# Scores in pieces of 512 keys, transposed rows as one transfer, first weights in the gather ring: one change to a one-core inference step

## The reference, cut to what matters

```
h = rmsnorm(x) * g1;  z = h @ w_in                        # D = 1024, w_in is 1024 x 3096
GLA heads (4): gated linear attention with a decaying state; output normed, times silu(gate)
FoX heads (8 of 64): s = q.k/8 + c_q - c_k (c = running sum of log forget gates), causal softmax, @ v
x = x + concat(GLA, FoX) @ w_out
PEER: q = rmsnorm(x)*g2 @ w_q (8 heads); scores of 2 x 128 subkeys, top 16 of each, top 16 of the 256 sums;
      idx -> rows u, v of 16384 experts;  x = x + sum over 128 picks of softmax(top)*gelu(u.h)*v
```

## Time and profile before

| what | us |
|---|---|
| median of 3 runs (3266.09 to 3274.44) | 3267.21 |
| the profiled execution | 3259.53 |
| its span, first to last instruction | 3257.7 |
| first gather issued, after the start | 149.0 |

### The profile page before, as it was taken

How to read it: one execution, slowest core, us unless ns; L and a number is a source line. 1 busy time by engine, 2 the same in 40 slices (tenths; PEclk the granted TensorE clock), 3 DMA queues, 4 the chain that set the end, 5 groups by cost and what they waited for, 6 DMA issues and landing times. The chain is left out here.

```text
span 3257.7 us, 34318 instructions
## 1 busy us (share of the span) xinstructions
PE 2673.6 (82%) x9396; PEld 1587.3 (49%) x9396; DVE 2528.8 (78%) x5522; ACT 1489.3 (46%) x3922; POOL 1290.6 (40%) x1062
## 2 busy tenths in 40 slices
PE   7768788886987888787977898888887898888777
PEld 5647456443753455444643455444643446444322
DVE  2498887999668768997677777998668766888864
ACT  2252463454235744454245654444245663444532
POOL 0024333443344434334443443444444434444443
PEclk9789758998998999998988899998998999988889
DMA  6499988999999999999999899999999999999998
GB/s 219 153 410 398 375 328 340 421 421 404 398 421 398 420 395 395 418 415 394 421 417 374 354 407 410 415 421 404 422 418 380 415 369 406 416 420 418 408 421 352
DMA packets 193753, 1269.82 MB, mean 390 GB/s; under 512 B 23720, under 2 KB 36792, under 8 KB 43032
## 3 DMA queue, kind: packets, MB, share of 16 engines
q0 software_dynamic: 152064, 1107.36, 83.4%
q1 hardware_dynamic: 36712, 154.26, 11.9%
q10 hardware_dynamic: 4784, 6.01, 0.6%
HBM read 1258.55 MB, written 9.00 MB: 389 GB/s over the span
## 5 line engine op out<-in xcount | busy, mean ns | idle before, releaser
L734 POOL DMA_INDIRECT uv_ring<-in_peer_uv,expert_index x1056 | 1285.8, 1218 | 1944.3 <-PE ps_acc L1301 1491.6
L1301 PE MATMUL ps_acc<-uv_ring,coef_diag 128*128 128x512 f32 x2744 | 1455.7, 672 | 451.1 <-ACT coef_diag L1000 430.5
L1662 DVE CUSTOM_DVE_ANT_0 uv_ring<-uv_ring,h_rows 128x1024 f32<-128x1024 f32 x1056 | 1281.7, 1220 | 357.5 <-DMA uv_ring<-in_peer_uv,expert_index 347.9
L1301 PEld LDWEIGHTS ps_acc<-uv_ring,coef_diag 128*128 128x128 f32 x2744 | 552.1, 212 | 1113.3 <-ACT coef_diag L1000 569.5
L995 ACT ACTIVATE gelu_u_dot_h<-u_dot_h 128x2 f32<-128x2 f32 x528 | 107.2, 203 | 1370.0 <-DVE u_dot_h L1662 1363.5
L1676 DVE SCALAR_TENSOR_TENSOR v_sums<-uv_ring,coefficients,v_sums 128x1024 f32<-128x1024 f32 x362 | 464.3, 1283 | 47.5 <-ACT coefficients L1002 42.9
L1072 PE MATMUL ps_scores<-weight_chunk,rows_T 128*128 128x256 f32 x1728 | 395.3, 384 | 18.8 <-DMA weight_chunk<-in_w_in_chunks 18.7
L1072 PEld LDWEIGHTS ps_scores<-weight_chunk,rows_T 128*128 128x128 f32 x1728 | 329.1, 192 | 98.9 <-issue 32.7
L1259 PE MATMUL ps_turn<-rows_T,weight_chunk 128*128 128x256 f32 (+1 forms) x1280 | 265.6, 362 | 2.7 <-ACT rows_T L902 2.6
L1000 ACT ACTIVATE coef_diag<-coef_diag,gelu_u_dot_h 128x128 f32<-128x128 f32 x686 | 254.8, 397 | 16.6
L1259 PEld LDWEIGHTS ps_turn<-rows_T,weight_chunk 128*128 128x128 f32 x1280 | 226.8, 194 | 54.5 <-issue 30.8
(11 more groups left out here) (190 smaller groups left out, 2175.8 us busy)
## 6 DMA issues: line engine op xcount, KB each, us to landing
weight_chunk<-in_w_in_chunks SPq DMA_DIRECT2D x60, 1024.0 KB
weight_chunk<-in_w_peer_q_and_subkeys SPq DMA_DIRECT2D x40, 1152.0 KB
weight_chunk<-in_w_out_chunks SPq DMA_DIRECT2D x20, 1024.0 KB
uv_ring<-in_peer_uv,expert_index POOLq DMA_INDIRECT x1056
rows_T<-in_x_T SPq DMA_DIRECT2D x9, 512.0 KB, 44.0
mix_rows<-in_x_rows SPq DMA_DIRECT2D x9, 512.0 KB
x_mid<-in_x_rows SPq DMA_DIRECT2D x9, 512.0 KB, 13.6
out_y_p<-v_sums ACTq DMA_DIRECT2D x8, 512.0 KB
```

Of the source, the lines that this page charges most:

```text
L734: pool.indirect_dma_start(out=ring[:, s % RING, :], out_offset=None, in_=dram["uv"], in_offset=bass.IndirectOffsetOnAxis(ap=idx[:, t % IDX ...
L1301: mm = pe.matmul(acc[:, c, :], diag[:, r, :], ring[:, r, D + c * 512:D + (c + 1) * 512], start=first, stop=False, skip_group_check=True)
L1662: dve.tensor_tensor_reduce(out=ring[:, s % RING, 0:D], in0=ring[:, s % RING, 0:D], in1=h2[:], scale=1.0, scalar=0.0, op0=ALU.mult, op1=ALU ...
```

## The change

1. **Scores in pieces** (tiles 4 to 8). A head's scores are made, reduced and exponentiated in pieces of up to 512 keys, each in the next of three banks; a second small VectorE reduction joins the maxima, a last one adds the row sums. The steps are laid out anew: 47 to 62 steps in a tile of attention, where there were 32 or 33.
2. **One transfer of transposed rows per batch**, contiguous per partition, issued by ScalarE behind the copy of the last PEER query. The rows are no longer loaded into `mix_rows`: ScalarE squares the transposed rows into it, and TensorE sums over the partitions with a column of ones (16 matmul instructions of one column per tile, as the page counts two instructions for each float32 matmul). `x_std` and `x_rstd` move to a later step.
3. **First weights in the ring.** Chunks 0 to 7 of batch 0 go to the ring's 8 places, 8 and 9 to the two buffers, 10 to 15 (the last two of w_in and all of w_out) to places 0 to 5 again; from then on the two buffers serve as before.
4. **Constants.** `ident`, `tri`, `fold`, `less` and `iota` are one packed transfer; 5 transfers are waited for by TensorE and VectorE, 4 more by VectorE's first `gla` step, and the rest is issued by SyncE ahead of chunk 10. The sums of the past are made later, partly inside `gla` of tile 0.

```diff
+def at_step(t, what, h, x):
+    n = quads(t)
+    if not wide(t):                      # wide(t): t >= 4
+        return lag(t) * (2 + what) + 3 * h
+    after = [2, 4, 4 + n, 6 + n, 10 - n // 3 + n, 12 - n // 3 + n]   # SCORE, MAX, EXP, TURN, COPY, VALUE
+    return after[what] + 2 * n * h + x
@@ weights
+    def weights(n):
+        if n < RING:
+            return ring[:, n, :], first_in[n], 16
+        if RING + WBUF <= n < RING_END:
+            r = n - RING - WBUF
+            return ring[:, r, :], first_in[r], 32
+        m = n - RING if n < RING_END else n - RING_END + WBUF
+        return wb[m % WBUF][:], wb_in[m % WBUF], 16 * (m // WBUF + 1)
@@ scalar, mix_front
-  act.wait_ge(xr_in[i], 16 * (round_of(t) + 1))
-  act.activation(mix[i][:], mix[i][:], ACT.Square, accum_out=ss[:, i:i + 1]).then_inc(x_sq, 1)
-  act.activation(std[:, i:i + 1], ss[:, i:i + 1], ACT.Sqrt, bias=eps[:], scale=1.0 / D).then_inc(x_std, 1)
+  act.wait_ge(xT_in, 16 * (bi + 1))
+  wait(act, q_t, fills_before(t0))
+  act.activation(mix[i][:].rearrange("p (k t) -> p k t", k=KD), xT(t), ACT.Square).then_inc(x_sq, 1)
+  if step == n + 2:
+      for i, t in enumerate(ts):
+          act.wait_ge(x_ss, t0 + n)
+          act.activation(std[:, i:i + 1], ss_ps[i], ACT.Sqrt, bias=eps[:], scale=1.0 / D).then_inc(x_std, 1)
@@ tensor, mix_front, step n + 1, behind the small projection and ahead of chunk 0
+  if bi == 0:
+      pe.wait_ge(cst, 16 * EARLY)        # EARLY = 5, it was 11
+  for i, t in enumerate(ts):
+      pe.wait_ge(x_sq, t + 1)
+      for k in range(KD):
+          mm = pe.matmul(ss_ps[i], mix[i][:, k * P:(k + 1) * P], ones, start=(k == 0), stop=(k == KD - 1), ...)
+      mm.then_inc(x_ss, 1)
@@ scalar, route, behind the copy of the last query
+  act.dma_start(xT_flat[:, 0:KD * len(BATCHES[bi + 1]) * P], dram["xT"][bi + 1]).then_inc(xT_in, 16)
@@ tensor, scores of one piece
-    wait(pe, ex, FH * t + max(h - heads_in_flight(t) + 1, 0))
+    wait(pe, ex, pieces_before(t) + max(h * quads(t) + x - 2, 0))
@@ vector, attend
-  dve.tensor_reduce(nm[h % 2][:], S[:, lo:lo + total], AX.X, ALU.max, negate=True).then_inc(nm_r, 1)
+  dve.tensor_reduce(nmp[:, h % 2, x:x + 1], score_piece(t, h, x), AX.X, ALU.max, negate=True).then_inc(nmp_r, 1)
+  if x == quads(t) - 1:
+      dve.tensor_reduce(nm[h % 2][:], nmp[:, h % 2, 0:x + 1], AX.X, ALU.min).then_inc(nm_r, 1)
@@ vector, mix_front
-  dve.tensor_tensor(xT[i], xT[i], g1[:]..., ALU.mult).then_inc(x_g, 1)
+  dve.wait_ge(x_sq, t + 1)
+  dve.tensor_tensor(xT(t), xT(t), g1[:]..., ALU.mult).then_inc(x_g, 1)
```

More of the change, by code:

```diff
@@ L166, in lag, with wide, due_steps, pieces_before @@
     return 2 if t < 4 else 1
+def wide(t):
+    return t >= 4
+SCORE, MAX, EXP, TURN, COPY, VALUE = range(6)
+def at_step(t, what, h, x):
[4 more added lines that the diff above has]
+    return after[what] + 2 * n * h + x
+def due_steps(t, what):
+    return {at_step(t, what, h, x): (h, x) for h in range(FH) for x in range(quads(t))}
 def value_at(t):
-    return 7 * lag(t) + 3 * (FH - 1) + (quads(t) - 1) // 2
+    return at_step(t, VALUE, FH - 1, quads(t) - 1)
 def att_steps(t):
     return value_at(t) + 3 * lag(t) + 1
+def pieces_before(t):
+    return FH * sum(quads(u) for u in range(t))
+def piece(t, h, x):
+    return pieces_before(t) + h * quads(t) + x
 def key_blocks(t):
@@ L612, in chunk @@
             n = CHUNKS * bi + c
-            b = n % WBUF
-            if n >= WBUF:
-                bu, cu = divmod(n - WBUF, CHUNKS)
+            to, here, _ = weights(n)
+            last = None
+            if n >= RING_END + WBUF:
+                last = n - WBUF
+            elif n >= RING_END:
+                last = n - RING_END + RING
+            elif n >= RING + WBUF:
+                last = n - RING - WBUF
+            if last is not None:
+                bu, cu = divmod(last, CHUNKS)
                 tiles = len(BATCHES[bu])
@@ L691, in _ @@
                 chunk(bi, 0)
-                rows(bi, ts)
             else:
                 chunk(bi, 0)
-                turned_rows(bi, ts)
             for c in range(1, IN_CH):
+                if bi == 0 and c == RING + WBUF:
+                    constants()
                 chunk(bi, c)
-            for c in range(IN_CH, IN_CH + WBUF):
+            ahead = (OUT_CH if bi == 0 else 0) + WBUF
+            for c in range(IN_CH, IN_CH + ahead):
                 chunk(bi, c)
@@ L706, in _ @@
                 cache()
-            for c in range(IN_CH + WBUF, IN_CH + OUT_CH + WBUF):
+            for c in range(IN_CH + ahead, CHUNKS):
                 chunk(bi, c)
[L709 to L712, removed]
         for i in range(NB):
@@ L1063, in mix_front @@
                     chunk = CHUNKS * bi + c
+                    w, here, loads = weights(chunk)
                     if i == 0:
-                        pe.wait_ge(wb_in[chunk % WBUF], 16 * (chunk // WBUF + 1))
+                        pe.wait_ge(here, loads)
                     if u == 0:
```

270 lines of the change are left out of this document (140 added, 130 removed).

## The result

The changed kernel takes 3286.2 us (20 runs, 3272.2 to 3301.3) against 3262.5 for the kernel before (20 runs): ratio 1.0067 with a 95% interval of 1.0057 to 1.0078, so 0.67% slower, outside the range of 3226 to 3275. The profiled execution took 3289.68 us (span 3287.8; before 3259.53 and 3257.7). Between these two executions lie 30.1 us, between the medians 23.7, as the one of before was 3.0 us under its median and the one of after 3.5 over.

The account below looks back on a forecast made before the run. The prediction took DMA as the bound of the gather stream, with small holes, behind a serial prologue. It summed -10 - 15 + 11 - 3 = -17 from 3259.5 to 3242.5, plus 7.7 for the median: 3250, range 3226 to 3275.

Parts of the forecast that it names:

- Prologue, -10: Before the first gather: waits for weights go and chunk 0 begins at 15.3, 10 us less (bounds 3 and 14).
- DMA work, -15: Beside the gathers: row loads into `mix_rows` go, 10 us, and transposed rows come in larger pieces, 5 us.
- all 15 us count: Both transfers ran beside gathers in stages with full DMA, so the whole 15 us saved shortens the kernel.
- a share under 0.98 in the routing stages: Sign of being wrong: the DMA share in route stages falling under 0.98.
- the 5 us for larger pieces: Transposed rows in 8 KB instead of 512 B pieces: 5.7 us less DMA work, taken as 5.
- Starts of batches, +11: At four batch starts, 32 matmuls each ahead of chunk 0 add 14.4 us, less a wait of 3.0: net 11.
- one for one: At batch starts the ring has no slack, so TensorE time ahead of chunk 0 goes fully to the end: 14.4 us.
- The credit of 3 for batch 1: At batch 1's start VectorE's wait of 3.0 us goes, set against the 14.4 us.
- The bound of 28: Worse end for batch starts: 28 us more, if the waits for `x_std` and `x_rstd` hold up as much again.
- Attention, -3: Tiles 4 to 8: scores filled ahead close DMA holes, 3 us less (bounds 15.5 off and 34 more).
- third rival: Late attention: ScalarE becomes the bound as gelus part the exps, table loads delaying adds; +20, 3287 us; chance 0.12.
- second rival: Whole kernel: freed DMA time turns into holes and each batch start costs 5; -4, 3263 us; chance 0.20.

Follow-up runs that it names:

- both_undone: Changed kernel with tile 8's attention as before in one group and, from batch 1 on, the norm from loaded rows: 3250.4 us, ratio to before 0.9968.
- ones_wide: As ones_idle, but each unread matmul moves 128 columns instead of one: 3264.0 us, ratio to before 1.0019.
- ones_idle: both_undone with, from batch 1 on, the one-column matmuls put back ahead of chunk 0, results unread: 3272.0 us, ratio to before 1.0045.
- att8_one_group: Changed kernel with only tile 8's attention laid out as before, one score product, maximum and exp per head: 3269.3 us, ratio to before 1.0024.
- att8_steps: Changed kernel with only the three-piece step list altered, to 2, 4, 7, 9, 10, 11: 3276.2 us, ratio to before 1.0053.
- first_sums_wide: both_undone with batch 0's sums of squares moving 128 columns instead of one: 3253.2 us, ratio to before 0.9975.
- ones_later: att8_one_group with, from batch 1 on, the sums placed behind chunk 0 (first tile) and the next product (second): 3255.1 us, ratio to before 0.9991.

## Why the prediction was wrong

**Prologue, -10: right.** Measured -11.0, by the steps given: no waits for weights in the projection, chunk 0 at 15.2. That is the faster of the two forms; in the slower one, which half of the ten profiles have, the first gather is only 5.3 to 7.3 us earlier than before.

**DMA work, -15: right in size, and half of it did not reach the end.** By the profile's page q1 and q10 had 11.9 and 0.6% of 3257.7 us before, 11.1 and 0.8% of 3287.8 after: 16 us less, but the rounding of four shares can move this by up to 6. The stages away from the starts and late attention are only 7.6 us shorter, so the step "all 15 us count" does not hold. The sign named for it, a share under 0.98 in the routing stages, did not come: it is 1.01 there. With both parts undone the bytes behind the first gather are those of before again (1244.33 MB), and the time is too (3110.4 against 3108.7 us), so the 5 us for larger pieces are not shown.

**Starts of batches, +11: the step that failed.** The step read "32 x 0.111 = 3.6 us: four starts, 14.4 us ... Net 11". 3.6 was near (3.73, and 4.28 where the clock fell within them), but the four starts cost 28.5. Step by step through the runs that is 2.1 from before to both_undone, 13.8 from there to ones_wide, 4.7 to ones_idle and 7.9 to the changed kernel. The 13.8 are the "one for one" of the forecast, for 15.4 us of matmuls (4 x 3.84). Missing was the clock: the chunks behind the block run in part at half of it (1.5 to 1.7 us more at three batches, 2.8 at one). In ones_idle, whose batch 1 is spared, that makes the 4.7; by the timed runs of ones_idle against ones_wide it is 8. The 7.9 are what waits and the scatter of batch 1 have between them. The credit of 3 for batch 1 had the wrong sign: that window grew most, by 13.0, or by 7.0 as att8_one_group has it. The bound of 28 had the size by luck: it was given for waits, which are the smaller part.

**Attention, -3: the second step that failed.** The step summed instructions, let the loop "scores, maximum, exp, scores" lose some 2 us in a round, and never walked the list of steps for three pieces. The wait of TensorE's scores for an exp was only 9.7 us in the whole kernel before, and grew to 13.3, of which tile 8 has 11.6; that growth was a sign named for being wrong. Tiles 7 and 8 cost 21.3 us, of which tile 8's list of steps has 12 to 13 (att8_steps, att8_one_group); pieces in tiles 4 to 7 are worth 5 at most and show no gain. ScalarE did become busier, 45 us over the kernel with 14 more table loads for exp and 14 for gelu; in tile 8 that was harmless, as att8_steps shows. So the third rival had the right sign and time (3287) by luck, by a mechanism that isn't there.

**The sum** by measured stages: -11.0 for the prologue, +28.5 for the starts, +21.3 for tiles 7 and 8, -1.1 for tiles 5 and 6, -7.6 for the rest is +30.1, the growth of the span; the -7.6 is the remainder, so that this sum closes by construction. Two small slips changed nothing: the 7.7 us added for the median of three runs are 3.0 with twenty, and the second rival's four starts at 5 us less the 3 of batch 1 make 17, not 16. Why tile 7 takes 7.3 us more is not settled. With tile 8 mended it took 96.4, and with tiles 4 to 7 in one group 92.4, as the 92.0 before; in the changed kernel TensorE's turns wait 9.0 us for ScalarE's copies in it, a wait that its profile before does not list. The forecast's chance of 0.11 for slower came from asking what bounds late attention, and not what each added instruction stands in front of.

## What to carry to other kernels

Count what stands between two services of the resource that is full, here two adds that free ring slots, and not the work added: the same 32 matmuls cost 28 us as a block ahead of a chunk, with the clock that they took along, and 9 when split. When a pattern of software steps gets a new period or one more piece, write out for each step what it waits for and at which step that is done, for the largest case: here another list alone took 12 us off one tile. And where a sum over partitions needs a column of ones, try a block of 128 columns too: here it cost 0.11 us for 32 matmuls, and the chunk behind it was not slowed.

## What the runs showed of the hardware

A block of 32 matmuls with 128x128 weights takes 3.73 us with one moving column and 3.84 with 128, so the columns hardly count; in the block of batch 3 the weight loads are busy for 4.19 of its 4.28 us. At the block with one column, with TensorE busy throughout, the granted clock fell from 1.00 to 0.50, and in batches 2 to 4 the next 16 matmuls took 5.16 to 6.63 us instead of 3.72 (12 of 12 starts in four profiles; at batch 1, 3 of 4 were slow). Behind that with 128 columns they took 3.62, and so they did behind 16 with one column that have adds behind them; the granted clock was 1.00 over them at batch 3 of each. The clock is lowered at other places too: the small projection of batch 3 took 4.64 us instead of 3.67 in first_sums_wide, at a granted clock of 0.78, with no such block near it. In the slow prologues 48 matmuls took 13.52 us with a recorded clock of 1.00 throughout (this is ones_later, TensorE alone), so there the record does not show what the durations do:

```profile
16.70:30.10 13.40, 13.40 (x49) 1.00 1.01 419
```
